# A hybrid decoder step on one core: the mix reads its input from SBUF, the memory is prepared in the output job, its key products run between the mix's products, and two norms scale the products instead of their inputs

## What is computed

```
h = rmsnorm(x, norm_mix); u = h @ w_in                # three token mixers read slices of u
merged = g0 * b_lru + g1 * b_gla + g2 * b_ssd         # g = sigmoid(gate logits), b_ssd = y @ w_ssd_out
x = x + merged @ w_mix_out
mn = rmsnorm(mem, norm_mem); K = mn @ w_xk; V = mn @ w_xv     # mem: 256 tokens; K and V are outputs too
x = x + softmax((rmsnorm(x, norm_xattn) @ w_xq) @ K^T / 16) @ V @ w_xo
h = rmsnorm(x, norm_ffn)
x = x + (silu(h @ w_gate) * (h @ w_up)) @ w_down      # 2816 columns between
y = rmsnorm(x, norm_final)
```

## Time and profile before

| | |
|---|---|
| median of 3 runs | 3081.6 us (3078.11 to 3083.63) |
| the profiled execution | 3082.17 us, its span 3080.5 us |
| PE busy | 2929.0 us, 95% of the span |
| DVE, ACT, POOL busy | 1199.1, 708.8, 824.7 us |
| mean granted clock of TensorE | 0.977 |

### The profile page before, as it was taken

One profiled execution on the slowest core, in us unless ns is written; L12 is line 12 of the kernel. 1 busy time (PEld: TensorE's weight loads), 2 busy tenths in 40 slices (PEclk: granted clock), 3 DMA queues, 4 the chain that ended last, 5 costly groups with the idle time before them and its releaser, 6 DMA issues. The chain is left out here.

```text
span 3080.5 us, 41502 instructions
## 1 busy us (share of the span) xinstructions
PE 2929.0 (95%) x17754; PEld 2746.7 (89%) x17754; DVE 1199.1 (39%) x1840; ACT 708.8 (23%) x1309; POOL 824.7 (27%) x493
## 2 busy tenths in 40 slices
PE   7999999999999999989988997998989999999997
PEld 6998999797888899977758997987989999999997
DVE  5886002324233257328832316024253222222225
ACT  3554001222121112225521223133020000000002
POOL 3332322121221223234322215301222323232320
PEclk9999999999999999999989998999999999999999
DMA  3111222211122432222234524252111111111111
GB/s 111 42 35 38 70 63 61 67 47 59 40 73 61 162 116 76 73 87 78 86 89 157 171 64 116 62 164 76 42 35 49 42 48 42 46 44 44 46 43 71
DMA packets 301976, 223.05 MB, mean 72 GB/s; under 512 B 30939, under 2 KB 279836, under 8 KB 301794
## 3 DMA queue, kind: packets, MB, share of 16 engines
q1 hardware_dynamic: 225602, 132.21, 15.2%
q10 hardware_dynamic: 76192, 88.19, 8.7%
HBM read 176.30 MB, written 44.07 MB: 72 GB/s over the span
## 5 line engine op out<-in xcount | busy, mean ns | idle before, releaser
L734 PE MATMUL PS<-Hh,Wh 128*128 128x384 f32 (+1 forms) x2928 | 965.2, 330 | 7.4 <-ACT WK L1421 6.0
L734 PE MATMUL PS<-Hh,Wl 128*128 128x384 f32 (+1 forms) x2928 | 959.4, 328 | 0.0
L734 PE MATMUL PS<-Hl,Wh 128*128 128x384 f32 (+1 forms) x2928 | 959.0, 328 | 0.0
L674 POOL CAST Wh<-Wr 128x1024 fp32r<-128x1024 f32 x197 | 217.5, 1104 | 1959.2 <-DMA Wr<-in_w_in 816.9
L734 PEld LDWEIGHTS PS<-Hh,Wh 128*128 128x128 f32 x2928 | 553.3, 189 | 9.9 <-POOL Wl L676 6.5
L676 POOL TENSOR_TENSOR Wl<-Wr,Wh 128x1024 fp32r<-128x1024 f32 x213 | 536.8, 2521 | 83.6 <-ACT Wh L2000 67.8
L734 PEld LDWEIGHTS PS<-Hl,Wh 128*128 128x128 f32 x2928 | 553.2, 189 | 0.6
L734 PEld LDWEIGHTS PS<-Hh,Wl 128*128 128x128 f32 x2928 | 552.7, 189 | 0.0
L2189 DVE SCALAR_TENSOR_TENSOR WK<-WK,PS 128x384 f32<-128x384 f32 (+1 forms) x252 | 133.2, 532 | 873.8 <-PE PS L734 495.6
L2805 DVE TENSOR_TENSOR X<-X,PS 128x384 f32<-128x384 f32 (+1 forms) x288 | 149.6, 532 | 167.0 <-PE PS L1384 89.7
L734 PE MATMUL PS<-Yh,Wh 128*128 128x384 f32 (+1 forms) x576 | 189.2, 329 | 4.8 <-DVE Yl L2465 4.8
(11 more groups left out here) (414 smaller groups left out, 4109.7 us busy)
## 6 DMA issues: line engine op xcount, KB each, us to landing
Wr<-in_w_in SPq DMA_DIRECT2D x82, 512.0 KB, 3.9
merged<-WK ACTq DMA_DIRECT2D x22, 544.0 KB, 3.9
WK<-merged ACTq DMA_DIRECT2D x22, 544.0 KB, 5.9
Wr<-in_w_ffn_gate SPq DMA_DIRECT2D x22, 512.0 KB, 3.7
Wr<-in_w_ffn_up SPq DMA_DIRECT2D x22, 512.0 KB, 3.8
Wr<-in_w_ffn_down SPq DMA_DIRECT2D x22, 512.0 KB, 3.7
WK<-gates ACTq DMA_DIRECT2D x16, 544.0 KB, 5.2
Wr<-in_w_lru_out SPq DMA_DIRECT2D x8, 512.0 KB, 4.4
```

The lines of the kernel that those rows point to most:

```text
L674: pool.tensor_copy(Wh[:, n % SLOTS], Wr[:, n % SLOTS]).then_inc(w_hi, 1)
L734: mm = pe.matmul(bank(f"{name}:{g}")[:, 0:n], L[:, w % SLOTS, k, :], R[:, k, t0:t0 + n], start=(k == 0 and i == 0), stop=(last and k == DT ...
```

## The change

1. The sum of each tile of output job 2 is no longer stored: ACT copies it to Hh (`hi_sum`) and DVE subtracts (`lo_sum`) within the same job. MI, `put` and `get` of this job go. XT is loaded once ob2_7 is done.
2. The memory is loaded ahead of the job's first gate, into another buffer (MR); its root is taken by ACT after the second tanh, it is scaled by DVE after the third tile and turned by PE behind ob2_3, weighted in place. Hi and lo follow once the job has ended.
3. The key products run behind the mix products, one after each; POOL makes the hi parts of their weights too. The value products follow the mix.
4. The norm ahead of the attention: Hh and Hl are made of X * gain only (`hi_scaled` on ACT, `lo_scaled` on DVE), in between the value products; DVE multiplies the query products by the token factor SQ as it empties the banks.
5. The norm ahead of the FFN the same way: PE starts fg0_0 and fu0_0 without the factor, sums the squares ahead of their k steps 3 and 5 (`sum_norm`, into PM, a PSUM tensor outside the ring), and DVE multiplies the gate product (before the tanh, which is now one operation per tile) and the gated up product (h times SQ) by SQ.

The diff, cut to its core:

```diff
@@ plan
             use([(name, t * P)], f"ob{b}_{t}")
+            if b == 2 and t == 3:
+                banks("mt0", 2)
+                banks("mt1", 2)
...
         use([("mix", t * P)], f"mx{t}")
-        if t in (4, 5):
-            banks(f"mt{t - 4}", 2)
+        use([("xk", t * P)], f"mk{t}", n=1)
     for t in range(DT):
-        use([("xk", t * P)], f"mk{t}", n=1)
+        use([("xv", t * P)], f"mv{t}", n=1)
+        if t == 0:
+            banks("kt0", 2)
         if t == 1:
             banks("xn")
...
-    banks("fn")
@@ POOL, split_to
-                    if WLIST[n][0] not in ("xk", "xv"):
+                    if WLIST[n][0] != "xv":
                         pool.tensor_copy(Wh[:, n % SLOTS], Wr[:, n % SLOTS]).then_inc(w_hi, 1)
@@ PE
-                if t in (4, 5):
-                    turn_memory(t - 4)
-
-            pe.wait_ge(S("mem_lo"), 2)
-            for t in range(DT):
+                pe.wait_ge(S("mem_lo"), 2)
                 project_memory(f"mk{t}", FIRST_W["xk", t * P])
...
+            def sum_norm(parts):
+                for i in parts:
+                    t0, n = SUM_GROUPS[i]
+                    pe.wait_ge(S("nrm_sum"), NSUM * 2)
+                    if i == 2:
+                        pe.wait_ge(S("nrm_std"), 1)
+                    pe.matmul(PM[:, i % 2, 0:n], ones[:], SQ[:, t0:t0 + n], start=True, stop=True)\
+                        .then_inc(S("nrm_mm"), 1)
...
-                        project_by_tile(("fg0_0", "fu0_0"), FIRST_W["fg", 0], ("nrm_lo", DT))
+                        project_by_tile(("fg0_0", "fu0_0"), FIRST_W["fg", 0], ("nrm_lo", DT),
+                                        {3: lambda: sum_norm((0, 1)), 5: lambda: sum_norm((2,))})
@@ ACT, output job and mix
+                def hi_sum(t):
+                    act.wait_ge(S("m_new"), b * DT + t + 1)
+                    act.activation(Hh[:, t], wk(4 + t % 2)[:, 0:T], ACT.Copy).then_inc(S("mi_hi"), 1)
...
+                    if b == 2:
+                        act.dma_start(MR, I["mem_prompt"][0].rearrange("(m p) f -> p m f", p=P)).then_inc(S("mem_in"), 16)
                     get_gate(0)
...
-                        if t and (b == 1 or t <= DT - 2):
+                        if t and b == 1:
                             put(t - 1)
...
+                        elif t:
+                            hi_sum(t - 1)
+                        if t and t + 1 < DT:
+                            get_gate(t + 1)
+                        if b == 2 and t == 1:
+                            memory_root()
...
+            ready(act, f"ob2_{DT - 1}:2")
             load_xt(0)
             load_xt(1)
...
+            def hi_scaled(k, row):
+                act.activation(Hh[:, k], X[:, k], ACT.Copy, scale=PV[:, k, row:row + 1]).then_inc(S("nrm_hi"), 1)
             for t in range(DT):
                 all_groups(f"mx{t}", X[:, t], ACT.Copy)
                 if t + 2 < DT:
                     load_xt(t + 2)
+                if t == 0:
+                    act.wait_ge(S("mem_lo"), 2)
                 square(0, t)
...
+                copy_product(f"mk{t}", KT_m[:, t])
@@ ACT, value products
+            for t in range(DT):
+                if t == 4:
                     ready(act, "vt0:1")
+                copy_product(f"mv{t}", VF[:, t % 4])
+                if t + SLOTS < DT:
                     hi_weights(w0 + t + SLOTS)
+                hi_scaled(t, R_NX)
+                if t == 0:
+                    copy_turned_kv("kt0", KM[:, :, 0:512])
                 if t == 1:
                     roots("xn")
@@ ACT, norm ahead of the FFN
+                if t < DT - 1:
+                    square(1, t)
             for k in range(DT):
+                hi_scaled(k, R_NFFN)
+                if k == 2:
+                    square(1, DT - 1)
@@ DVE
+            def lo_scaled(i, k, row):
+                dve.wait_ge(S("nrm_hi"), DT * i + k + 1)
+                stt(Hl[:, k], X[:, k], PV[:, k, row:row + 1], Hh[:, k].bitcast(F32), MUL, SUB).then_inc(S("nrm_lo"), 1)
+            for k in range(1, DT):
                 add_square(0, k)
...
+                lo_scaled(0, k, R_NX)
+                if k == 3:
+                    inverses("xn")
+
+            dve.wait_ge(stored, 16 * n_kv[0])
+            for t in range(DT):
+                for g, (t0, n) in enumerate(GROUPS):
+                    name = f"xq{t}:{g}"
+                    ready(dve, name)
+                    freed(dve.tensor_tensor(Q[:, t, t0:t0 + n], bank(name)[:, 0:n], SQ[:, t0:t0 + n], MUL), name)
...
+            for k in range(DT):
+                lo_scaled(1, k, R_NFFN)
+                if k == 2:
+                    add_square(1, DT - 1)
+            for i, (t0, n) in enumerate(SUM_GROUPS):
+                dve.wait_ge(S("nrm_std"), i + 1)
+                link(dve.reciprocal(SQ[:, t0:t0 + n], SQ[:, t0:t0 + n]))
@@ DVE, FFN
-                        dve.wait_ge(S("f_th"), 3 * q + g + 1)
-                        freed(stt(h[:, t0:t0 + n], h[:, t0:t0 + n], 1.0, bank(name)[:, 0:n], ADD, MUL), name)
+                        ready(dve, name)
+                        freed(dve.tensor_tensor(z[:, t0:t0 + n], bank(name)[:, 0:n], SQ[:, t0:t0 + n], MUL), name)
+                    dve.wait_ge(S("f_th"), q + 1)
+                    link(stt(h, h, 1.0, z, ADD, MUL))
...
+                    dve.tensor_tensor(h, h, SQ, MUL).then_inc(S("f_h"), 1)
                     dve.wait_ge(S("f_hi"), q + 1)
```

## The result

The changed kernel took 3061.2 us (median of 5 runs, 3056.4 to 3069.7) beside 3081.7 us (5 runs, 3078.1 to 3086.6): a ratio of 0.9934, 95% interval 0.9914 to 0.9954. That is 20.5 us, with 14 to 27 in the interval. The profiled execution took 3061.2 us, its span was 3059.5 us, against 3080.5 before: 20.9 us less. The forecast was 3060.0.

The account below looks back on a forecast made before the run. TensorE is busy 95% of the span, so only its idle and slow-clock time can be won. Terms 6.1 + 5.4 + 10.7 = 22.2 us off the profiled 3082.17 us give 3060.0 us, range 3051 to 3072.

Parts of the forecast that it names:

- the memory's: Key and value products of the memory: 80.93 us becomes 75.5, 5.4 us won, range -3 to +9.
- The mix's input: First mix tile, mx0: no wait on low parts left and no slow clock, 17.95 us becomes 11.88, 6.1 us won.
- Rival D: Mix: mx0 still waits as much as before, with a gate load or XT late; 3066 us, chance 0.04.
- The key products in the mix: Mix: 8 key products of 3.15 us, 25.2 us in all, a mix period of 17.4 us, no wait.
- The value products: From the end of mk7 to the first query product: 50.3 us, still bound by the weights.
- The account of ACT's queue: Value products: ACT's program order makes PE wait 4.1 us ahead of mv0, 4.0 at vt0, 2.3 ahead of mv4.
- I take 1, since only four low parts fall there: Ahead of the queries: DVE's low parts beside POOL's weight splits lengthen the stretch by 1 us.
- The norm: Ahead of the FFN: PE starts 3.2 us behind xo7, 10.7 us won, slow clock at the start left as is.
- The FFN: FFN passes: two more full-width DVE operations per tile cost nothing, with 0.7 us of cover ahead of the down product.
- Rival A: FFN: Fl comes behind POOL's cast and subtract, PE waits 3.1 us in each of 11 passes; 3094 us, chance 0.06.
- B: Value products win nothing because ACT's queue is later than counted; 3065.4 us, up to 3070, chance 0.17.
- C: Gaps of 3 us keep the clock, 2.2 us at the FFN's start and 2.3 at mv4; 3055.5 us, chance 0.12.

Follow-up runs that it names:

- the last kernel above: Changed kernel with ACT reordered, DVE's reciprocals later, and also the high part of the first value weights made inside mx7, ahead of its copies: 3047.4 us, ratio 0.9883.
- the one before it: Changed kernel with another order of ACT's instructions (high parts of X in its waits for weight loads) and DVE's reciprocals behind low part 6: 3047.8 us, ratio 0.9899.

## Why the prediction was right, point by point

The total was 3060.0, the measurement 3061.2, and every term but the memory's has the right size. The two errors in that one should be learned from; that they don't show in the total is in part luck, as told at the end of this section.

**The mix's input**: forecast 6.1 us, 5.9 in the rows of the changed kernel and of both profiles of the part alone. No wait on a low part is left, XT came without a wait, and the first tanh, behind the memory's load 2.2 us later in its job than before, made PE wait for nothing. Rival D, a wait left in mx0, didn't come. The timed gain of this part alone is smaller than its rows, as told above.

**The key products in the mix**: forecast at 3.15 us each, a period of 17.4, and 139 us from ob2_7 to the end of mk7. They took 3.07 each, a period of 17.07, and 136.7 us in all. The turns of the memory moved rather than went, as forecast: ob2 is 1.7 us longer, the mix 2.1 shorter for them.

**The value products**: forecast 50.3 us, measured 54.3. The account of ACT's queue held in the main: wait ahead of mv0 4.1 forecast, 3.9 measured; vt0 4.0 and 2.8; mv4 2.3 and 3.2; mv4's start 29.5 and 30.6 us behind mk7. The 1.1 us are the smaller error: the count let PE run from mv0 to mv3 without a stop, but it waited 1.1 us for the kt0 copies ahead of mv2 and 1.3 for the roots ahead of mv3. So mv3 ended at 23.6 instead of 22.1, the load of xv6 came later with it, and ACT waited 1.2 us for that load ahead of the vt0 copies. PE's waits in the stretch (us in total, times, longest):

```profile
PE PS L774 <- POOL Wl L676: 6.1, 1, 6.1
PE PS L1191 <- POOL Wl L676: 5.7, 2, 3.9
PE PS L798 <- ACT WK L1996: 3.3, 2, 2.8
PE PS L1191 <- ACT WK L2018: 3.2, 1, 3.2
PE PS L1191 <- ACT WK L1986: 1.3, 1, 1.3
PE PS L1191 <- ACT KM L2018: 1.1, 1, 1.1
```

The failed step, and the larger error, is "I take 1, since only four low parts fall there". It leaned on the mean excess of POOL's subtracts; but that is a mean over 18 subtracts, of which eleven took 2.34 to 2.41 us and seven 2.57 to 3.51. What counts is how many of DVE's operations stand ready beside POOL's queue. With four ready, they take turns, and each made one operation of POOL about 1 us longer, casts too: 3.95 us. With one left beside the five operations (the last kernel above) the queries waited 1.0 us more than with none (the one before it). The Trainium skill (SBUF — State Buffer, SBUF: two separate sides) describes the port pair, for a VectorE operation with two inputs in SBUF beside one of GpSimd that reads SBUF, as an exclusive lock, which the operation that starts first keeps. The rows agree in all three places: the subtract beside Fl took 3.31 us, Fl behind the subtract 3.29, and in turns a cast 2.10 and a subtract 3.29.

The Trainium skill's drain of about 1.38 us beside each table load (ScalarE: Activation LUTs, What ACT_TABLE_LOAD costs), weighed in the prediction, is not in these rows. ACT's chain has the load of 1.28 between a high part that ends at 1888.67 and the roots at 1889.99:

```profile
1887.58 1.09 ACT Hh L2000
...
1888.69 1.28 ACT L1986
...
1889.99 0.59 ACT WK L1986
```

**The norm**: forecast 10.7 us and a start 3.2 us behind xo7; measured 10.75 and 3.37. The slow clock behind the shorter gap stayed in this profile (0.94 over 27.67 us), as forecast, but that was luck: in the second profile of the same kernel, behind the same gap, it is 1.00 over 26.14 us, and the part gives 12.3 us.

**The FFN**: forecast at nothing with 0.7 us of cover; the pass is 71.28 us as before, and the kernel with one more operation puts the cover at 0.9: the first bank is emptied at E + 4.9, where 5.2 was counted. The end E of the up product is at 2410.44 here. DVE, then POOL:

```profile
2411.09 1.29 DVE L2859 TENSOR_TENSOR WK<-WK 128x1088 f32<-128x1088 f32 x1
2413.57 1.29 DVE L2861 TENSOR_TENSOR Fl<-WK,Fh 128x1088 fp32r<-128x1088 f32 x1 [1.18 <-ACT Fh L2165]
...
2414.26 1.51 POOL L674 CAST Wh<-Wr 128x1024 fp32r<-128x1024 f32 x1 [8.48 <-DMA Wr<-in_w_ffn_gate]
```

Fl starts at E + 3.13, the cast at E + 3.82 and takes 1.51 instead of 1.04, since DVE was first. Rival A, at 0.06, named the right mechanism; its price of 3.1 us a pass was low beside 3.7, and it had no clock in it. It needs Fl behind the subtract, and in the changed kernel Fl is over before the subtract starts: with one operation more it was 0.45 us ahead, with two 0.20 behind.

**The rivals' shares.** B, the value products win nothing, came half true: they and the key products gave 2.1 of 5.4 us. C, no slow clock, didn't come in the first profile: mv4 took 5.35 us behind a wait of 3.2, and mv0 4.62 behind one of 3.9; at the FFN's start it came in the second. The error of +3.3 in the memory's term was balanced by ob2 and the mix, which came out 1.4 us shorter together where no net was forecast, and by 1.4 in the attention and 0.3 in the queries, against 0.9 lost ahead of ob2. The attention and what lies ahead of ob2 are not the change's. So the closeness of the total, 1.2 us, is in part luck and says less than the single terms do.

## What to carry to other kernels

An engine that carries out several jobs in program order is worth a list of due times: here another order of ACT's instructions (and a later place for DVE's reciprocals) gave 12.6 us in the rows of its stretch, more than half of what the whole change gave, and the slow clock of mv4 and a port conflict went along with the waits. When two engines take turns at a port, count the operations that stand ready at the same time and price each, rather than spreading a mean excess over them. A cover of 0.9 us is enough as long as nothing else sits behind it: here a first operation of 1.29 us more cost 0.4 to 0.9 a pass, and a second one not 1.29 but 3.1, and the clock with it.

## What was not expected

Behind the waits of 0.4 to 0.9 us in the down products, and behind the one of 1.4 us ahead of mv4, no slow matmuls followed. Longer waits were mostly followed by them, but not always: mv4 took 5.50 us behind 2.3 in the second profile of the changed kernel, yet behind 2 of 10 waits of 3.72 us in the down products the clock held, and so it did behind the gap of 3.37 us in one of two profiles of the changed kernel. With two operations extra in the FFN this cost some 13 us on top of 37 us of waits.

The mix part gave 5.9 us in its rows and 2.4 and 3.4 in two timings; whether a part of it is lost elsewhere, these runs leave open.
